# Feed-forward output: sixteen of twenty-two gated blocks by seven-product groups, their token-side combinations formed on GpSimd

## What is computed

```python
h = rmsnorm(x, norm2_g[l]) * (1.0 + sc2) + sh2
gate, up = jnp.split(h @ w_ffn_in[l], 2, axis=-1)
x = x + gt2 * ((jax.nn.silu(gate) * up) @ w_ffn_out[l])
return rmsnorm(x, final_g)
```

## Time and profile before

| | |
|---|---|
| median of 3 runs | 1634.82 us (1634.08 to 1636.33) |
| profiled execution, span | 1634.9 us |
| gate/up stage, blocks 2 to 21 | 990 to 1376 us |
| output stage, 1056 matmuls | 1376 to 1621 us |
| last sums, scaling, transposes, stores | 1621 to 1634.9 us |
| TensorE busy | 1604.4 us (98%) |
| VectorE busy | 909.5 us (56%) |
| ScalarE busy | 640.9 us (39%) |
| GpSimd busy | 260.3 us (16%) |

### The profile page before, as it was taken

One profiled execution on the slowest core, in us unless ns is written; L12 is line 12 of the kernel. 1 busy time (PEld: TensorE's weight loads), 2 busy tenths in 40 slices (PEclk: granted clock), 3 DMA queues, 4 the chain that ended last, 5 costly groups with the idle time before them and its releaser, 6 DMA issues.

```text
span 1634.9 us, 23987 instructions
## 1 busy us (share of the span) xinstructions
PE 1604.4 (98%) x8239; PEld 1313.7 (80%) x8239; DVE 909.5 (56%) x1440; ACT 640.9 (39%) x1313; POOL 260.3 (16%) x282
## 2 busy tenths in 40 slices
PE   6999999999999999999999999999999999999998
PEld 5687878888877777878788888788888888888886
DVE  4576655435545454546652489766666666334424
ACT  4334456555544444444212244333333333232413
POOL 1036561011101010100000003223322220000000
PEclk9999999999999999999999999999999999999999
DMA  8826666655733333523545322322222224543412
GB/s 282 276 91 215 202 199 186 201 182 153 227 99 110 98 109 98 161 88 111 168 142 193 109 59 65 111 82 77 77 77 87 92 71 146 213 176 130 148 45 103
DMA packets 223678, 223.05 MB, mean 136 GB/s; under 512 B 19066, under 2 KB 189187, under 8 KB 223619
## 3 DMA queue, kind: packets, MB, share of 16 engines
q1 hardware_dynamic: 216642, 197.12, 37.7%
q0 software_dynamic: 6976, 25.17, 4.0%
HBM read 163.53 MB, written 60.31 MB: 137 GB/s over the span
## 4 chain that ended last, share of the span: by engine, by line
PE 87%; DVE 4%; DMA 3%; POOL 3%; SPq 1%; issue 1%; ACT 1%; DVEq 0%; POOLq 0%; ACTq 0%
PE pm L1642 22%; PE pm L1656 15%; PE ps L1211 13%; PE pd L1501 11%; PE pm L1211 8%; PE pm L1596 3%; PE sc L1454 2%; PE tT L1477 2%; PE tT L1466 2%; PE pm L1554 1%; POOL pr L1124 1%; POOL Xi L1126 1%; PE gps L1391 1%; DMA adab<-in_w_ada_dram 1%; DVE est L2311 1%
## 5 line engine op out<-in xcount | busy, mean ns | idle before, releaser
L1211 PE MATMUL ps<-act_hi,w_hi 128*128 128x512 f32 x448 | 150.0, 416 | 2.6 <-DVE est L2316 1.7
L2225 DVE TENSOR_TENSOR w_lo<-w_raw,w_hi 128x1024 fp32r<-128x1024 f32 x60 | 77.4, 1290 | 123.0 <-ACT w_hi L1751 113.2
L1211 PE MATMUL ps<-act_lo,w_hi 128*128 128x512 f32 x448 | 138.9, 391 | 0.0
L1211 PE MATMUL ps<-act_hi,w_lo 128*128 128x512 f32 x448 | 138.5, 390 | 0.0
L1656 PE MATMUL pm<-act_hi,w_hi 128*128 128x512 f32 x352 | 137.2, 390 | 0.0
L1656 PE MATMUL pm<-act_hi,w_lo 128*128 128x512 f32 x352 | 137.0, 389 | 0.0
L1656 PE MATMUL pm<-act_lo,w_hi 128*128 128x512 f32 x352 | 136.9, 389 | 0.0
L1642 PE MATMUL pm<-act_hi,w_hi 128*128 128x512 f32 x320 | 124.5, 389 | 0.0
L1642 PE MATMUL pm<-act_lo,w_hi 128*128 128x512 f32 x320 | 124.5, 389 | 0.0
L1642 PE MATMUL pm<-act_hi,w_lo 128*128 128x512 f32 x320 | 124.5, 389 | 0.0
L1501 PE MATMUL pd<-act_hi,w_hi 128*128 128x512 f32 x256 | 111.3, 435 | 0.0
(11 more groups left out here) (375 smaller groups left out, 3462.0 us busy)
## 6 DMA issues: line engine op xcount, KB each, us to landing
w_raw<-in_w_in_dram SPq DMA_DIRECT2D x44, 512.0 KB, 5.3
w_raw<-in_w_ffn_in_dram SPq DMA_DIRECT2D x44, 512.0 KB, 3.7
h_raw<-h_d SPq DMA_DIRECT2D x36, 512.0 KB, 3.4
a_raw<-in_w_ada_dram SPq DMA_DIRECT2D x32, 512.0 KB, 4.2
w_raw<-in_w_ffn_out_dram SPq DMA_DIRECT2D x44, 256.0 KB, 3.8
h_d<-hid SPq DMA_DIRECT2D x21, 512.0 KB, 2.7
pk_d<-pk SPq DMA_DIRECT2D x8, 768.0 KB, 3.7
qkva_d<-est POOLq DMA_DIRECT2D x12, 512.0 KB, 6.0
```

What stands on the lines that cost most here:

```text
L1211: ins = pe.matmul(dst[:, cols], wt[:, ds % 2, k, :], at[:, cols], start=(first and n == 0), stop=(last and n == 2))
L2225: dve.tensor_tensor(w_lo[:, ds % 2], w_raw[:, ds % NR], w_hi[:, ds % 2].bitcast(F32), ALU.subtract)\
```

## The change

Of the 22 gated blocks, 16 (2 to 17) are multiplied with `w_ffn_out` by the same seven products as gate/up; 0, 1 and 18 to 21 stay direct.

- Two groups of eight blocks. In a group the pairs (2,3), (4,5), ... are the two halves of the contraction; two column blocks at a time make a unit. Four units a group: n = 22 to 25 is group 0, n = 26 to 29 group 1. `product` runs on for n = 22 to 29: 8 x 84 = 672 matmuls. Then come 12 direct steps (`NF` = 6 for each half of the columns): 288. Together 960 instead of 1056.
- Token-side combinations (four of 128x512 for each pair) are formed in the gate/up loop by GpSimd (`mix_hidden`, 4 operations for each two blocks, 32 in all) and stored to `tq_d` (eight stores of 1 MB). VectorE's product into `hid` waits for them.
- The operands of a group are 28 *quarters* of 128x512 (7 products x 4): 12 from `h_d`, 16 from `tq_d`. `load_quarter` brings each through a ring of six buffers; `quarter_hi` splits on ScalarE; `quarter_lo` on VectorE for three of four, on GpSimd for each fourth. ScalarE and VectorE do them over twelve steps from step (21, P1) for group 0 and from step (25, P1) for group 1, in the numbers of `PACE`. Quarters 0 to 3 belong to P1, 4 to 7 to P2, and so on. `product` of n = 22 and n = 26 waits for them (`hlo_ready`, `hlo_pool`).
- GpSimd also does `mix_weights` for n = 22 to 29; its quarters of a group stand behind `mix_weights(22)` (four of them) and behind `mix_weights(23)` (three), or behind those of 26 and 27.
- From n = 22 on, `op_hi`/`op_lo` work four products ahead instead of seven, in four buffers.
- Sums go to `xF`. In group 0 as in gate/up (six and `add_mid`), in group 1 `out_sums` adds to what is there: ten operations and `add_mid`, each waiting for the one before.
- In block 29 the six direct blocks are loaded whole and split (`chunk_hi`, `chunk_lo`, 128x1024). After it VectorE adds x (eight 128x1024 operations over `x2s`, with `o_lo(4)` to `o_lo(7)` between), then does `o_lo(8)` to `o_lo(11)`, then the eight `residual` of the first half of the columns. The loads of x wait for the last product of block 29. `o_hi(11)` waits for direct step 5.

The core of the diff:

```diff
+        def step_slot(t):
+
+            if t in (8, 9):
+                return w3_hi[:, t - 8], w3_lo[:, t - 8]
+            s = t % 4 if t < 8 else t - 10
+            return quarter(w_hi, s), quarter(w_lo, s)
...
             sp.wait_ge(h_ready, 1)
             sp.dma_start(h_d[0:P, :], tmp[:, :]).then_inc(h_stored[0], 16)
-            with sp.Fori(0, 9) as i:
-                for n in (4, 5):
-                    load_gate_up(n, i, i * (2 * P) + n * P)
-                    store_h(n - 3, i, i * (2 * P) + (n - 3) * P)
+            for n in (4, 5):
+                load_gate_up(n, 0, n * P)
+                store_h(n - 3, 0, (n - 3) * P)
+
+            def store_mixed(i):
+
+                sp.wait_ge(tq_ready, 4 * i + LEAD)
+                sp.dma_start(tq_d[bass.ds(i, 1)].rearrange("a m p c -> (a p) m c"), tq).then_inc(tq_stored, 16)
+
+            with sp.Fori(1, 9) as i:
+                load_gate_up(4, i, i * (2 * P) + 4 * P)
+                store_h(1, i, i * (2 * P) + P)
+                load_gate_up(5, i, i * (2 * P) + 5 * P)
+                store_mixed(i)
+                store_h(2, i, i * (2 * P) + 2 * P)
+
...
-            def load_h(x):
-
-                j = block_of(H_SPLITS[x])
-                if x >= 3:
-                    sp.wait_ge(hlo_ready, x - 2)
-                sp.wait_ge(h_stored[j % 2], 16 * (j // 2 + 1))
-                sp.dma_start(h_raw[:, x % 3, :], h_d[j * P:(j + 1) * P, :]).then_inc(y_in[x % 3], 16)
+            def load_quarter(x):
+
+                g, o, c, y = quarter_of(x)
+                pair = 4 * g + c
+                if y >= 6:
+                    sp.wait_ge(*quarter_done(x - 6))
+                elif g == 0:
+                    sp.wait_ge(tq_stored, 16 * 10)
+                else:
+                    sp.wait_ge(dense_mm, op_count(N_OUT - 1, O_P5))
+                    sp.wait_ge(*quarter_done(x - 28 + (24 if y < 4 else 18)))
+                n = 2 + 2 * pair
+                if o in (O_P1, O_P2, O_P3):
+                    n += o != O_P1
+                    sp.wait_ge(h_stored[n % 2], 16 * (n // 2 + 1))
+                    src = h_d[n * P:(n + 1) * P, half(o == O_P3)]
+                else:
+                    src = tq_d[pair + 1, {O_P5: 0, O_P6: 1, O_P7: 2, O_P4: 3}[o]]
+                sp.dma_start(quarter_raw(x), src).then_inc(hq_in[y % 6], 16)
...
-            for u in range(3):
-                load_h(u)
-            for t in range(4, 7):
+            load_quarters(0, 6, 18)
+            load_out(24, 0)
+            load_quarters(0, 18, 24)
+            store_h(21, 0, 21 * P)
+            load_quarters(0, 24, 28)
+            load_out(24, 1)
+            load_out(25, 0)
+            load_quarters(1, 0, 6)
+            load_out(25, 1)
+            for n in (26, 27):
+                for e in range(2):
+                    load_out(n, e)
+            load_quarters(1, 6, 18)
+            load_out(28, 0)
+            load_quarters(1, 18, 28)
+            load_out(28, 1)
+            load_out(29, 0)
+            for j in range(3):
+                load_chunk(j)
+            load_out(29, 1)
...
                 load_o(t)
-            load_h(3)
-            store_h(21, 0, 21 * P)
-            for t in range(7, STEPS):
+            load_chunk(3)
+            load_o(4)
+            load_chunk(4)
+            load_o(5)
+            load_chunk(5)
+            sp.wait_ge(xT_stored, 16 * 11)
+            sp.wait_ge(dense_mm, step_count(-1))
+            for b in range(4):
+                load_x2(b)
+            load_o(6)
+            load_o(7)
+            sp.wait_ge(xT_in, 16 * 5)
+            for b in range(4, 8):
+                load_x2(b)
+            for t in range(8, STEPS):
                 load_o(t)
-                if t < NF + 6 or NF + 9 <= t < STEPS - 2:
-                    load_h(t - (3 if t < NF + 6 else 6))
...
-                    mix_weights(n, i, wait_apart)
-            mix_weights(21)
+            pool.sem_inc(tq_ready, LEAD)
+
+            def mix_hidden(i):
+
+                b11, b12, b21, b22 = (hid[:, n, half(h)] for n in range(2) for h in range(2))
+                t1, t2, t3, t4 = (tq[:, m, :] for m in range(4))
+                wait_apart(h_ready, 2 * i + 2)
+                wait_apart(tq_stored, 16 * i + 16)
+                pool.tensor_tensor(t1, b12, b11, ALU.subtract).then_inc(tq_ready, 1)
+                pool.tensor_tensor(t3, b22, b12, ALU.subtract).then_inc(tq_ready, 1)
+                wait_apart(tq_ready, 4 * i - 2 + LEAD)
+                pool.tensor_tensor(t2, b22, t1, ALU.subtract).then_inc(tq_ready, 1)
+                wait_apart(tq_ready, 4 * i - 1 + LEAD)
+                pool.tensor_tensor(t4, b21, t2, ALU.subtract).then_inc(tq_ready, 1)
...
+            with pool.Fori(1, 9) as i:
+                mix_weights(3, i, wait_apart)
+                mix_hidden(i)
+                mix_weights(4, i, wait_apart)
+            pool.wait_ge(tq_ready, 4 * 8 + LEAD)
+            pool.sem_inc(tq_ready, 4)
+
+            def quarter_lo(x):
+
+                g, o, c, y = quarter_of(x)
+                hi, lo = operand(o, c)
+                pool.wait_ge(hhi_ready, x + 1)
+                pool.tensor_tensor(lo, quarter_raw(x), hi.bitcast(F32), ALU.subtract).then_inc(hlo_pool, 1)
+
+            for n in range(21, N_END):
+                mix_weights(n)
+                for grp in range(2):
+                    if n in (N_OUT + 4 * grp, N_OUT + 4 * grp + 1):
+                        for k in range(4) if n == N_OUT + 4 * grp else range(4, 7):
...
+                if n in (N_OUT, N_OUT + 4):
+                    k = 7 * (n > N_OUT) + OP_ORDER.index(o)
+                    pe.wait_ge(hlo_ready, 3 * k + 3)
+                    pe.wait_ge(hlo_pool, HP + k + 1)
+                whi, wlo = slot_of(n, o)
...
+                elif n >= N_OUT:
+                    act.wait_ge(dense_mm, op_count(n, o) - 4)
...
 
-                if t >= 7:
-                    act.wait_ge(dense_mm, step_count(t - 7))
+                if t in (8, 9):
+                    act.wait_ge(hlo_ready, ALL_DVE + NF)
                 else:
-                    act.wait_ge(dense_mm, op_count(NF - 1, t))
+                    act.wait_ge(dense_mm, step_count(t - 4 if t < 8 else t - 6))
...
+            def ahead_hi(n, o):
+
+                n2, o2 = divmod(7 * n + o + 4, 7)
+                if n2 == N_END:
+                    o_hi(o2)
+                elif n2 >= N_OUT:
+                    op_hi(n2, o2)
+                for g in range(2):
+                    k = 7 * (n - (N_OUT - 1 + 4 * g)) + o
+                    if 0 <= k < len(PACE):
+                        for y in paced(k):
+                            quarter_hi(QUARTERS * g + y)
...
+                    if n >= 3:
+                        dve.wait_ge(tq_ready, 4 * ((n - 2) // 2) + 4 * i + LEAD)
...
+            def out_sums(n, o):
+
+                b0 = 2 * ((n - N_OUT) % 4)
+                g0, g1, u0, u1 = (xF[:, b, half(h)] for b in (b0, b0 + 1) for h in range(2))
+
+                def bring(j, count, dst, other, last=False):
+
+                    if count is not None:
+                        dve.wait_ge(*count)
+                    ins = dve.tensor_tensor(dst, dst, other, ALU.add)
+                    if last:
+                        ins.then_inc(sum_ready, 1)
+                        dve.wait_ge(sum_ready, sum_count(n, j))
+                    else:
+                        ch.link(ins)
+
+                if o == O_P2:
+                    bring(None, (part_read, part_count(n, 1)), g0, p1)
+                    bring(SUM_11, (dense_mm, op_count(n, O_P2)), g0, bank(n, O_P2), True)
+                if o == O_P6:
+                    bring(None, (mid_ready, n - 1), g1, q6)
+                    bring(SUM_U4, (part_read, part_count(n, 2)), g1, p5, True)
+                if o == O_P3:
+                    bring(SUM_12, (dense_mm, op_count(n, O_P3)), g1, bank(n, O_P3), True)
+                if o == O_P7:
+                    bring(SUM_U3, (dense_mm, op_count(n, O_P7)), q6, bank(n, O_P7), True)
+                    bring(None, None, u0, q6)
+                    bring(None, None, u1, q6)
+                    bring(SUM_22, None, u1, p5, True)
+                if o == O_P4:
+                    bring(SUM_21, (dense_mm, op_count(n, O_P4)), u0, bank(n, O_P4), True)
...
+            hidden(21, 0, lambda o: ahead_lo(21, o))
+            for n in range(N_OUT, N_END):
+                for o in range(7):
+                    if o == O_P6:
+                        add_mid(n)
+                    if n >= N_OUT + 4:
+                        out_sums(n, o)
+                    else:
+                        for j in SUMS_AT.get(o, ()):
+                            add_parts(n, j)
+                    ahead_lo(n, o)
+            for b in range(KT):
+                dve.wait_ge(xT_in, 16 * (5 if b < 4 else 9))
+                ch.link(dve.scalar_tensor_tensor(xF[:, b, :], xF[:, b, :], gt2h[:, b:b + 1], x2s[:, b, :],
```

(14 more changed lines are left out.)

270 lines of the change are left out of this document (173 added, 97 removed).

## The result

| | before | changed |
|---|---|---|
| median | 1635.6 us (4 runs) | 1646.4 us (4 runs, 1645.9 to 1647.6) |
| ratio, 95% interval | | 1.0069, 1.0057 to 1.0081 |
| span of the profiled execution | 1634.9 us | 1644.2 us |

What follows compares the result with a forecast made beforehand. The output stage was taken as bound by TensorE's number of matmuls. 1634.9 - 21.8 + 10.1 + 14.3 + 3.4 + 4.5 = 1645.4 us; own range 1638 to 1652 (chance 0.48), 8-in-10 range 1624 to 1656.

Steps and rivals of the forecast that it cites:

- eight places of a wait: TensorE waits forecast at (22, P3), (22, P4), (25, P7), (26, P3), (26, P7), (26, P4), direct step 0, direct step 6.
- 96 matmuls: Output stage: 960 matmuls instead of 1056, at 0.2266 us each, saves 21.8 us.
- group 0, to (22, P4): Blocks 21 and 22: VectorE's last needed quarter comes at 45.0 us, TensorE wants it at 34.9: +10.1 us.
- group 1, to (26, P4): Blocks 25 and 26: late quarter 6 and GpSimd's locks, last quarter at 49.2 us against 34.9: +14.3 us.
- block 29: First direct step's second token half waits for SUM_21, behind VectorE's chunk splits: +3.4 us, between 2 and 6.
- between the halves: Between the column halves, residuals stand behind o_lo(11), which needs step 5 complete; fourth column block late: +4.5 us.
- rival (1): GpSimd's operations fall into VectorE's gaps and PSUM reads, only order costs: 1624.0 us; decides at (22, P3); chance 0.18.
- landing 2.7: Group 1's quarter 6: two transfers at once were taken to land 2.7 us after issue, delaying add_mid(25).
- The clock: TensorE at half clock for 8 matmuls after a long wait, 1.6 us more; counted in groups 0 and 1.
- Rival (3): Clock falls after every wait over 2 us, four more times 1.6 us, and locks in full: 1659 us; chance 0.16.
- Rival (2): Only half of the locks on VectorE's port cost time: 1634 us, near no change; chance 0.12.
- Rival (4): Token combinations delay the gate/up loop by one GpSimd operation per pair, 10 us in all: 1656 us; chance 0.04.

Runs made afterwards that it cites:

- pool_small: Changed kernel with every GpSimd operation from block 22's weight combinations on cut to 8 columns, results incomplete, a price only: 1633.6 us (one run).
- sum_first: Changed kernel with VectorE's chunk splits in block 29 one step later, so the last sums come first: 1643.47 us, 1.0050 of before.
- vector_quarters: Changed kernel with GpSimd's 14 quarters done by VectorE, in their places by number: 1643.47 us, 1.0051 of before.
- residual_first: Changed kernel with o_lo(11) placed behind the eight residuals: 1643.54 us, 1.0052 of before.
- vector_both: Changed kernel with GpSimd's quarters and mix_weights(23) and (27) on VectorE, the latter behind its last quarter: 1635.93 us, 1.0004 of before.
- sp_order: Changed kernel with quarters 6 to 9 of group 1 loaded ahead of the second half of block 27's weights: 1640.74 us, 1.0037 of before.
- pool_order: Changed kernel with all seven GpSimd quarters of a group ahead of mix_weights of its second block: 1640.0 us, 1.0022 of before.

## Why the prediction was right, and where it was not

The sign, the size (1646.4 for 1645), and seven of the eight places of a wait came as forecast. The eighth, (26, P7) behind `add_mid`, has none, and direct step 6 has one wait instead of four. The size is right in part by luck, as the terms show; here they stand against the traces, as delays of the start that follows:

| term | predicted | measured |
|---|---|---|
| 96 matmuls | -21.8 | -21.8 (at the old cadence) |
| ahead of the change (execution) | 0 | -1.7 |
| gate/up, early wait | 0 | -1.0 |
| group 0, to (22, P4) | +10.1 | +8.3 |
| group 1, to (26, P4) | +14.3 | +13.7 |
| half clock behind (26, P4) | 0 | +1.7 |
| block 29 | +3.4 | +5.1 |
| between the halves | +4.5 | +4.1 |

(Group 0: 4.50 + 1.79 + 2 x 0.16 + 1.7. Group 1: 4.68 + 2.05 + 2.92 + 3 x 0.16 + 2 x 1.7 = 13.5 by the waits, 13.7 by the start of P4. Block 29: 3.25 + 0.16 + 1.7. Halves: 2.20 + 0.16 + 1.7. The rows measured add up to 8.4, the spans to 9.3; 0.4 and 0.5 of the 0.9 between are the small wait at 1007.93 and the difference of 33.2 and 32.7 above.)

**Group 0** was right step by step, with each step somewhat shorter than forecast (the start of P3 4.7 us late for 6, that of P4 1.9 for 2.5). VectorE ended block 21's products at 1384.34 (1382.92 + 1.42), 28.3 us after the mark at 1356.0 (29.2 predicted; block 22's first matmul starts at 1374.62, which puts the mark a block of 19.04 earlier, plus 0.45). GpSimd's two combinations and quarter 19 took from 1385.09 to 1390.01, 4.9 us (5.4). It was to decide at 26 us for rival (1): at 28.3 that rival fell. pool_small shows the term's reason: without GpSimd's work (its hold on the port and its own time in the queue together) 8.3 us become 0.19 + 0.16, so its share is 8.0 (9.1 predicted, 10.1 less the 1 of a group without locks). That VectorE's splits stand still while GpSimd computes is what 1000 and 1258 ns against 686 and 685 say; the lock behaves as the Trainium skill, "SBUF — State Buffer", section "Who interferes with whom", has it.

**Group 1** was right in its sum and wrong inside. The step "landing 2.7" was too short: the two quarters landed 4.2 us after their issue, with half a block's weights issued right before them and further quarters behind. And 13.0 us for GpSimd's operations was too much: without them pool_small still has 3.73 + 1.09 us of waits, and a half clock that cost 2.6, in all 7.7 with 2 x 0.16, instead of 13.7. (The windows lose 3.4 there, but the clock is down from 1450.0 on and the first matmul starts at 1451.32, so that a part fell into the wait.) So GpSimd's share there was 6.0 us, where I had held 12.3 (14.3 less the "some 2" of a group without locks). A likely reason is that what the load holds up in block 25 the lock can't hold up again; no run tests it.

**The clock** is the term that was mis-sized most: I took two stretches at half clock (group 0, group 1), and there were six, 10.2 us instead of 3.2. Rival (3)'s four further stretches happened, its locks in full did not. That the sum was nevertheless right is due to waits that came shorter: 22.5 us where the same terms without clock make 29.1 (32.3 - 3.2). Two errors of some 7 us met, which is luck.

**Block 29** was inside its range (2 to 6); the missing part is the half clock. **Between the halves** the 4.5 us were forecast as wait alone; measured were 2.4 us of wait and 1.7 of clock, so that sum too is right by luck. The three further reads of PSUM, which I let TensorE wait for, show no waits in the changed kernel: behind 2.20 us the clock is 0.57 to 0.60, and TensorE comes to them later. In sum_first, where it is higher there (0.81), waits of 0.29 and 0.16 us are seen.

**The other rivals,** (2), half of the locks, and (4), token combinations delaying the loop, have to be told apart. Rival (2) was nearer to the lock's price than its chance said: the two shares above are 14.0 us, half clocks included, of the 21.4 (9.1 + 12.3) in my sum; its time of 1634 was not reached, with the other half clocks and the load on top. Rival (4) fell, since the gate/up stage keeps its pace: 1672 matmuls in 384 us, 0.2297 each, as 1679 in 386, 0.2299.

**What I had not asked**, and the runs show: the two kinds of GpSimd work differ. Quarters on it are worth no more than on VectorE; the combinations of weights for the second block, placed in the densest stretch, cost 6.0 to 7.5 us. By the prediction's price for one operation both would be alike. In vector_quarters the four combinations take 3.7 us from VectorE right ahead of an awaited split, with no quarter queued behind them, and the wait is 3.81; the hold on VectorE at that moment is thus enough. Why a quarter costs no more than it saves is open. Part of it may be that the first of a group come while VectorE still has gaps to take the loss: in the changed kernel the first, at 1361.25, is followed by 1.84 us in which VectorE waits for ScalarE.

## What to carry to other kernels

Before work goes to an idle engine, count what its instructions take from the busy one: next to a VectorE without gaps a GpSimd operation on SBUF is not free, and moving eight of them to VectorE, behind its urgent work, saved 6 to 7.5 us. Then look in each in-order queue at what stands ahead of the instruction that is awaited (a load behind weights, wide splits ahead of a sum, a split ahead of residuals): three such edits were worth 13 us, more than half of what the saved matmuls are. A saving on the bounding engine arrives only when the engines that feed it keep up in every stretch, and short waits can cost more than they show (1.7 us of half clock behind a wait of 2.05). And before two spans are balanced, look how far apart the two executions already are where the change begins.

## What was unexpected of the hardware

- The clock after a wait was less regular than one profile suggests. In the changed kernel it fell to 1.2 GHz, for a loss of 1.7 us, behind each wait from 2.05 to 4.68 us. But behind 3.81 us in vector_quarters, 3.25 in residual_first and 2.06 in vector_both the granted clock stayed at 1.00. In the edits' profiles a stretch loses 1.7, 3.4 or once 5.1 us in the windows (3.4 twice in pool_small and twice in sp_order, 5.1 around the wait of 7.13 in pool_order); in the longer ones the clock falls while TensorE still waits, and that part delays nothing. Behind 1.90 us it fell in sum_first and not in sp_order. So this term can differ by some us between edits that leave the waits alike, and a profile of one execution can't price it.
- The lock works both ways. In a stretch where both engines always have work, GpSimd's operation grows from 1.3 to 1.7 us too, as VectorE's split grows from 0.69 to 1.75: a pair in 1.7 us, where the two one after the other would be 0.60 + 1.29 = 1.9. So little is done side by side.
- Two transfers of 256 KB landed in 4.2 us with others in the queue; the page of the changed kernel has a median of 2.9 for the quarters from `tq_d`.
